# Chunked attention on one core: both heads' transposes behind the next scores, in three banks with three copies

## The reference

```python
# group A: 8 query heads on 2 key/value heads, own chunk + 1 before, with sinks
sc = einsum('bncvgd,bnlvd->bnvgcl', qc, kb) * HEAD_DIM ** -0.5
m = maximum(max(sc), sink);  p = exp(sc - m)
p = p / (sum(p) + exp(sink - m));  o = p @ vb
# group B: 8 heads, own chunk + 8 before, with a bias by relative position
sc = einsum('bnchd,bnlhd->bnhcl', qc, kb) * HEAD_DIM ** -0.5 + bias
p = softmax(sc);  o = p @ vb
```

## Time and profile before

| | us |
|---|---|
| median of 3 runs (2798.16 to 2803.1) | 2799.08 |
| the profiled execution | 2800.31 |
| its span | 2798.5 |
| TensorE busy | 2741.3 (98%) |
| VectorE busy | 1555.9 (56%) |
| ScalarE busy | 1091.2 (39%) |
| GpSimd busy | 1087.0 (39%) |
| first score of the attention stage | 534.46 |
| last values of the stage end | about 891.4 |
| mean granted TensorE clock | 0.993 of full |

### The profile page before, as it was taken

How to read it: one execution, slowest core, us unless ns; L and a number is a source line. 1 busy time by engine, 2 the same in 40 slices (tenths; PEclk the granted TensorE clock), 3 DMA queues, 4 the chain that set the end, 5 groups by cost and what they waited for, 6 DMA issues and landing times.

```text
span 2798.5 us, 41169 instructions
## 1 busy us (share of the span) xinstructions
PE 2741.3 (98%) x14774; PEld 2249.8 (80%) x14774; DVE 1555.9 (56%) x2465; ACT 1091.2 (39%) x2229; POOL 1087.0 (39%) x882
## 2 busy tenths in 40 slices
PE   9999999999999999999998999999999999999998
PEld 9888888777766788888886888887888887888876
DVE  3356664567676332333336666668766666654364
ACT  6434333377787223333325333334333332222342
POOL 7644454301011112311216555455655453552252
PEclk9999999999999999999999999999999999999999
DMA  8657868534366334022326333335333236544454
GB/s 280 235 179 254 267 210 272 172 125 140 115 184 216 135 132 173 32 89 80 91 64 225 113 98 102 98 99 199 120 110 98 90 110 213 219 145 148 139 171 136
DMA packets 260112, 425.45 MB, mean 152 GB/s; under 512 B 18256, under 2 KB 157520, under 8 KB 258896
## 3 DMA queue, kind: packets, MB, share of 16 engines
q1 hardware_dynamic: 222512, 355.29, 38.5%
q10 hardware_dynamic: 37408, 67.65, 7.8%
HBM read 282.35 MB, written 135.27 MB: 149 GB/s over the span
## 4 chain that ended last, share of the span: by engine, by line
PE 55%; DVE 2%; DMA 1%; POOL 1%; ACT 1%; issue 0%; SPq 0%; POOLq 0%; ACTq 0%; DVEq 0%
PE gu_acc L51 10%; PE gu_acc L52 10%; PE gu_acc L53 10%; PE down_acc L51 4%; PE down_acc L53 4%; PE down_acc L52 4%; PE cross_sum_o L51 2%; PE cross_sum_s L51 2%; PE cross_sum_s L53 2%; PE cross_sum_o L53 2%; PE cross_sum_o L52 2%; PE cross_sum_s L52 2%; PE cross_turned L2185 0%; PE cross_turned L1903 0%; DMA gu_t<-t_d 0%
## 5 line engine op out<-in xcount | busy, mean ns | idle before, releaser
L51 PE MATMUL gu_acc<-gu_t,shared_m 128*128 128x512 f32 x704 | 276.0, 392 | 5.0 <-DVE gu_t L2507 5.0
L52 PE MATMUL gu_acc<-gu_t,shared_m 128*128 128x512 f32 x704 | 275.0, 391 | 0.0
L53 PE MATMUL gu_acc<-gu_t,shared_m 128*128 128x512 f32 x704 | 274.9, 391 | 0.0
L350 POOL TENSOR_TENSOR front_wq_lo<-front_wq_raw,front_wq_hi 128x1024 fp32r<-128x1024 f32 x72 | 178.9, 2486 | 201.9 <-ACT front_wq_hi L346 201.7
L2450 ACT ACTIVATE shared_m<-kept_x 128x512 fp32r<-128x512 f32 x175 | 109.4, 628 | 210.8 <-PE gu_acc L53 187.8
L51 PEld LDWEIGHTS gu_acc<-gu_t,shared_m 128*128 128x128 f32 x704 | 132.8, 189 | 35.6 <-issue 4.7
L53 PEld LDWEIGHTS gu_acc<-gu_t,shared_m 128*128 128x128 f32 x704 | 132.7, 189 | 27.8
L52 PEld LDWEIGHTS gu_acc<-gu_t,shared_m 128*128 128x128 f32 x704 | 132.9, 189 | 27.3
L346 ACT ACTIVATE front_wq_hi<-front_wq_raw 128x1024 fp32r<-128x1024 f32 x72 | 76.2, 1058 | 187.0 <-PE qkv_acc L53 100.7
L51 PE MATMUL gu_acc<-shared_m 128*128 128x512 f32 x352 | 138.0, 392 | 2.9 <-POOL shared_m L2423 2.5
L53 PE MATMUL gu_acc<-shared_m 128*128 128x512 f32 x352 | 137.6, 391 | 0.0
(11 more groups left out here) (353 smaller groups left out, 7653.1 us busy)
## 6 DMA issues: line engine op xcount, KB each, us to landing
front_wq_raw<-in_w_in ACTq DMA_DIRECT2D x69, 512.0 KB, 4.0
head_h<-qk_d SPq DMA_DIRECT2D x48, 512.0 KB, 4.6
ahead_w_even<-in_w_gate SPq DMA_DIRECT2D x44, 512.0 KB, 4.5
kept_x<-in_w_up SPq DMA_DIRECT2D x44, 512.0 KB, 4.3
a_d<-gu_a_mix SPq DMA_DIRECT2D x88, 256.0 KB, 3.2
a_d<-gu_a SPq DMA_DIRECT2D x66, 256.0 KB, 4.2
kept_x<-in_w_down SPq DMA_DIRECT2D x56, 256.0 KB, 4.7
shared_m<-a_d SPq DMA_DIRECT2D x19, 704.0 KB, 4.2
```

The source lines that it names most:

```text
L51: pe.matmul(out, l_hi, r_hi, start=first, stop=False)
L52: pe.matmul(out, l_hi, r_lo, start=False, stop=False)
L53: return pe.matmul(out, l_lo, r_hi, start=False, stop=last)
L350: pool.tensor_tensor(self.lo[:, i % Q_SLOTS, :], self.raw[:, i % Q_SLOTS, :], raw(self.hi[:, i % Q_SLOTS, :]), ALU.subtract).then_inc(self ...
```

## The change

The transposes of both heads of a unit are now one block, issued behind the next scores, and land in three banks instead of two:

- `pieces(u)` takes the place of `blocks(u, x, piece)`. In a "b" unit bank 0 takes head 0's first four tiles, bank 1 head 1's, bank 2 the fifth tile of both heads. In an "a" unit all four tiles of both heads go to one bank, u modulo 3.
- `copier(u, j)` says who copies: in "b" units ScalarE bank 0 and VectorE bank 1; bank 2, and the one bank of an "a" unit, ScalarE in even units and VectorE in odd ones.
- TensorE's step: score(s), turn(s-2), turn_out(s-4), values(s-3).
- VectorE's step: the copies of s-2, divide(s-4), both maxima of s.
- ScalarE's step: copy_o(s-4), exp(s-1, 0), the copy of bank 0, exp(s-1, 1), the copy of bank 2 or of an "a" unit.
- The third bank is the one that `o_turned` had. The turned output now lies beside `sum_o` in one bank in "b" units, and in the unused second bank of `sum_s[0]` in "a" units. So values(u) also waits for the division of u-1 while u is at most `A0`.

```diff
-    def blocks(u, x, piece):
-        w = tiles(u)
+    def pieces(u):
         if is_a(u):
-            return range(w) if piece == x else range(0)
-        half = (w + 1) // 2
-        return range(0, half) if piece == 0 else range(half, w)
+            return ((u % 3, [(x, y) for x in range(2) for y in range(tiles(u))]),)
+        near, last = min(tiles(u), 4), [(x, 4) for x in range(2) if tiles(u) > 4]
+        return tuple((j, part) for j, part in ((0, [(0, y) for y in range(near)]),
+                                               (1, [(1, y) for y in range(near)]), (2, last)) if part)
...
+    def copier(u, j):
+        return ("act", "dve")[u % 2 if is_a(u) or j == 2 else j]
...
-        turned = [room.bank(f"turned{j}") for j in range(2)]
-        sum_o = room.bank("sum_o")
-        o_turned = room.bank("o_turned")
+        turned = [room.bank(f"turned{j}") for j in range(3)]
+        o_bank = room.bank("sum_o")
+        sum_o = o_bank[:, 0:P]
...
-        def copy(engine, instruction, u, x, piece):
-            if not len(blocks(u, x, piece)):
-                return
+        def copy(engine, instruction, u, j, part):
             after(engine, s_o, 2 * (u - 1))
-            engine.wait_ge(s_t[piece], pieces_before(u, x, piece) + 1)
+            engine.wait_ge(s_t[j], fillings(u, j) + 1)
...
+        def o_turned(u):
+            return sum_s[0][:, BANK:BANK + P] if is_a(u) else o_bank[:, P:2 * P]
...
                     if step >= 4:
                         copy_o(step - 4)
-                    if 2 <= step < NB + 2:
-                        copy(act, copied, step - 2, 0, 0)
                     if 1 <= step < NB + 1:
                         exp(step - 1, 0)
                     if 2 <= step < NB + 2:
-                        copy(act, copied, step - 2, 1, 0)
+                        copies(step - 2, False)
                     if 1 <= step < NB + 1:
                         exp(step - 1, 1)
+                    if 2 <= step < NB + 2:
+                        copies(step - 2, True)
...
-                for step in range(NB + 5):
-                    if step >= 5:
-                        divide(step - 5)
+                for step in range(NB + 4):
                     if 2 <= step < NB + 2:
-                        copy(dve, dve.tensor_copy, step - 2, 0, 1)
+                        for j, part in pieces(step - 2):
+                            if copier(step - 2, j) == "dve":
+                                copy(dve, dve.tensor_copy, step - 2, j, part)
+                    if step >= 4:
+                        divide(step - 4)
                     if step < NB:
                         maxima(step, 0)
                         maxima(step, 1)
-                    if 2 <= step < NB + 2:
-                        copy(dve, dve.tensor_copy, step - 2, 1, 1)
...
-                def turn(u, x):
+                def turn(u):
...
+                    for j, part in pieces(u):
+                        pe.wait_ge(s_exp, 2 * u + part[-1][0] + 1)
+                        after(pe, s_copied[j], fillings(u, j))
...
                 def values(u):
...
                     after(pe, s_o_sb, u)
+                    if u <= A0:
+                        after(pe, s_out, u)
...
                 for step in range(NB + 4):
-                    if 2 <= step < NB + 2:
-                        turn(step - 2, 0)
                     if step < NB:
                         score(step)
                     if 2 <= step < NB + 2:
-                        turn(step - 2, 1)
+                        turn(step - 2)
                     if step >= 4:
                         turn_out(step - 4)
                     if 3 <= step < NB + 3:
                         values(step - 3)
```

## The result

The changed kernel takes 3003.5 us (median of 4 runs, 2993.4 to 3005.6) against 2799.8 us of the kernel before: 1.0717 times as long, 95% interval 1.0704 to 1.0731. The profiled execution took 3005.6 us with a span of 3003.8. The forecast was slower, at 2940 us with a range of 2905 to 2990: the sign and the place of the loop were right, the size fell short by 63 us.

What follows compares the result with a forecast made beforehand. TensorE was taken to pace the attention stage, and after the change a loop through VectorE: 2800.3 us + 83 ("b" jobs) + 57 ("a" units) = 2940 us. The 8-in-10 range was 2905 to 2990 us.

Steps and rivals of the forecast that it cites:

- the loop: Attention stage: score, transposes, copy, division, maxima, next score run one behind the other; +83 us "b", +57 us "a".
- The 512-column copy: VectorE's copy in full "b" units: about 0.69 us, 0.60 to its follower; uncertainty -26 or +14 us overall.
- The short units: First six steps of each "b" job: the same loop with copies and maxima scaled to width, together 25.7 us.
- six handovers: Handovers in each of 128 units, estimated 0.05 us each, good to about 20 us either way.
- The change of shape: TensorE transposes: turning both heads together saves 0.09 us a unit, 12 us, worth nothing in TensorE's idle time.
- a rival with 0.11: Attention stage: TensorE's clock falls to half, doubling its terms; at half of the stage +100, 3040 us; chance 0.11.
- The other two rivals: Attention stage: TensorE stays the bound, 2788 us, chance 0.04; only "b" units bear the loop, 2883 us, chance 0.05.

Runs made afterwards that it cites:

- experiment 1: Changed kernel with VectorE's maxima of s ahead of the copies of s-2 and the division of s-4: 2898.1 us, 1.0354.
- experiment 2: Changed kernel with VectorE's order division of s-4, maxima of s, copies of s-2 last: 2877.3 us, 1.0260.
- experiment 3: As experiment 2, and on TensorE the output's turn of s-4 ahead of the transposes of s-2: 2792.7 us, 0.9970.
- experiment 8: Changed kernel with experiment 3's orders up to the first "a" units, from there experiment 1's: 2783.3 us, 0.9940.
- experiment 4: Changed kernel with four idle TensorE transposes behind the values of each "a" step: 2954.8 us, 1.0552.
- experiment 6: Changed kernel with two idle TensorE transposes, instead of four, in every "a" step: 2959.7 us, 1.0569.
- experiment 5: Changed kernel with four idle TensorE transposes a step in the last two "a" jobs only: 2979.7 us, 1.0638.

## Why the forecast was right about the cause and wrong about the size

**The loop** (forecast's centre): right, to within 0.04 us a unit. Full "b" units 5.03 and 5.37 us forecast, 5.06 and 5.39 measured; "a" units at the full clock 2.44 and 3.21, measured 2.43 and 3.25. The 512-column copy, not in the trace of before, was put at 0.69 us with 0.60 to its follower; it takes 0.69, and the reciprocal starts 0.61 behind it. One end was closer than forecast: the values were to be done 0.3 us ahead of the next score and were done 0.17 ahead, and experiment 1 shows what that wait costs once the maxima are out of its way. Experiments 2, 3 and 8 undo the loop step by step by order alone. With the clock taken out, it costs about 82 us in the "b" jobs (96 less the 14 below; 83 forecast) and 60 in the "a" jobs (experiment 4's 183.5 us of first-to-last score against 123.9; 57 forecast).

**The short units**: forecast 4.1, 4.5, 3.3, 3.9, 4.7, 5.0; measured in the profile 4.2, 4.6, 3.4, 3.9, then 5.5 and 6.8. The last two and the one after are the clock. TensorE in the second job, scores at 623.42, 627.33 and 632.87:

```profile
623.42 0.96 PE L1485 MATMUL att_sum_s<-head_h 64*128 64x512 f32 x6
...
627.33 1.31 PE L1485 MATMUL att_sum_s<-head_h 64*128 64x320 f32 x12 [0.78 <-DVE att_top L1428]
...
632.87 1.44 PE L1485 MATMUL att_sum_s<-head_h 64*128 64x320 f32 x8 [0.36 <-DVE att_top L1428]
```

```profile
624.00:628.00 4.00, 2.19 (x22) 1.00 0.79 211
628.00:632.00 4.00, 2.94 (x21) 0.52 0.71 247
```

The fifth to seventh unit of each job lose about 0.8, 1.7 and 0.9 us to it, 3.4 us a job, as the comparison in experiment 6 has it. Four jobs: some 14 us. (Two slips of the working changed nothing: these six forecasts add up to 25.5, not 25.7, and a bound of 0.05 us on six handovers in 128 units is 38 us, not 20.)

**The change of shape** that goes away was sized at 0.09 us a unit. Experiments 3 and 8 show 0.15: 3.82 to 3.67 in "b" units, 1.94 to 1.79 in "a" units. It lies in the transposes: in a full "b" unit the ten of them and the output's turn took 1.50 us from start to start before (0.60 + 0.21 + 0.69) and take 1.35 in experiment 8 (685.16 to 686.51). That it is the change of shape, and not something else of the one block, fits this but was not tested by itself. That it is hidden while the loop binds was right; freed of the loop it is worth the 18 us of experiment 8 (128 x 0.15 = 19).

**The clock is the step that failed.** The sum put it at nothing and left it to a rival with 0.11. The reason given was a reading of two rows: only one long gap lowers the clock, 2.51 us there, and my gaps of 1 to 1.5 us were safe. The runs show otherwise. Behind the stage's start (where a gap of 2.0 us stands in the kernel before as well) the changed kernel has no gap above 1.44 us ahead of its falls in the stage, and in experiment 2 it fell behind gaps of at most 0.78; and yet the clock fell, in every "b" job and nearly for good in the "a" jobs. Even the trace of before spoke against the reading. In the feed-forward stage the clock fell, for some 7 us (the stretch from 1512 to 1516 us stands at 0.68), behind two gaps of 1.06 us, the second of them in the first row here, and within the first 1.0 us of a third one of 1.94:

```profile
1505.89 1.09 PE L1903 MATMUL cross_turned<-kept_ident,cross_xn 128*128 128x128 f32 x8 [1.06 <-DVE cross_xn L2124]
1508.92 0.77 PE L51 MATMUL gu_acc<-gu_t,shared_m 128*128 128x512 f32 x1 [1.94 <-DVE gu_t L2507]
```

```profile
1508.00:1512.00 4.00, 3.08 (x7) 0.50 1.01 413
```

The part of the clock is about 49 us in the "a" jobs (experiment 4: 3003.5 - 2954.8) and 14 us in the "b" jobs, together nearly all of the 63 us missing.

The rival's price was too high, and where it hit, it hit in part by luck. It had doubled TensorE's terms; the rows last 1.7 times as long. For half of the stage at the low level it had +100 us, 3040 in all; the mean granted clock from 534 to 1092 us is 0.75, which is half of that time at the low level, and it cost 63. A full "b" unit was to take 7.9 us, 2.9 more than at the full clock; the sixth unit of a "b" job, all of it at the low level, takes 6.76, 1.7 more. An "a" unit was to take "about 3.7", and 3.36 and 4.08 have a mean of 3.72; but doubling the terms of the two sums gives 3.7 only for the even unit and 4.5 for the odd one.

The Trainium skill's rule, named in the forecast as the one for the rival (TensorE: Matmul & The Clock Gate, "A second HAM failure mode: psum-queue depth-cycling"), that repeated short idle times can make the clock swing, is borne out in the "b" jobs, which fall for 13.7 us each behind the first; in the "a" jobs the clock swung back only once, for 3.4 us in 58 units.

**The other two rivals** are out. TensorE doesn't stay the bound as the change stands: its scores are released by the maximum; it is the bound once the orders of experiment 8 are in. And the "a" units bear the loop in full.

**Open**: what in the idle time lowers the clock. Full "b" units of the changed kernel have gaps of 1.08 and 1.41 us, and from 657 to 692 us TensorE is busy only 25.07 of 35 us, at the full clock all the time. Those of experiment 1 have gaps of 1.59 and 1.92 us and see only short falls, of 3.4 or 6.8 us each. Experiment 2's "a" units, with 0.56 us, held for three jobs and then fell to the end of the stage. And the same short "b" units fell in the changed kernel and didn't in the second job of experiment 6. So neither the longest gap nor the idle share alone, as far as these runs go, says when it falls. Open too is why the clock comes back within two or three units in the "b" jobs (6.76, then 5.39), while the "a" units at the low clock keep it there with TensorE recorded busy for 18.18 of 20 us.

## What to carry to other kernels

Before reordering an engine's queue, write down for each instruction that releases the pacing engine what now stands ahead of it, and add up the loop from start to start: here three harmless-looking moves put transposes, a copy and a product between a score and its maxima, and the same banks with another order gain 0.6% instead of losing 7%. Put what releases the pacing engine first and the copies that are wanted a step later last, and look at each kind of unit by itself. And where a forecast leaves TensorE idle in every unit, price the half clock as a likely case, not as a remote one; before taking one gap of the trace as the limit, look up every stretch of it at the low clock and the gaps ahead of each.

## What the runs showed of the hardware that I had not expected

In the "a" jobs of the changed kernel the granted TensorE clock fell to 1.2 GHz with no idle time over 1.44 us ahead of the fall (1.6 at most later), in experiment 2 with none over 0.78 in the 67 us ahead of it. In the changed kernel it then stayed low for over 200 us but for 3.4, with TensorE recorded busy 16.5 to 18.2 of each 20 us. Four idle transposes a unit (0.43 us at the full clock) kept it at 2.4 GHz, from the start (experiment 4) or from the moment it had come back (experiment 5), and made the whole kernel 49 us shorter in experiment 4. The new arrangement of the transposes on TensorE is worth 0.15 us a unit, most likely for the one change of shape fewer between transposes and 64-row scores.
